# Convolution layer, first half: which engine makes the low halves of 14 weight units

## The chip, the cores and the metric

The kernel runs on one core of one Trainium2 chip. The core has five engines that run at the same time and wait for each other through semaphores: TensorE (PE, matrix products), VectorE (DVE), ScalarE (ACT), GpSimd (POOL) and SyncE (SP, which here only issues transfers). The metric is the device time of one execution in microseconds (us), as the median of several runs; lower is better.

## The reference, cut to what matters

The program computes two layers of a transformer-like network on 512 positions of width 1024: a first block (a gated delta-rule mixer, memory attention, a SwiGLU network), then a convolution layer with its SwiGLU network, then an attention layer with its own. The change touches the first half of the convolution layer: the product with `pw1_w`, the gate, and the depthwise convolution over 31 positions.

```python
def conformer_conv(x, norm_g, pw1_w, pw1_b, dw_w, dw_b, ln_g, ln_b, pw2_w, pw2_b):
    a, b = jnp.split(rmsnorm(x, norm_g) @ pw1_w + pw1_b, 2, axis=-1)
    h = a * jax.nn.sigmoid(b)
    h = lax.conv_general_dilated(
        h, dw_w[:, None, :], window_strides=(1,),
        padding=[(CONV_WIDTH - 1, 0)],
        dimension_numbers=('NWC', 'WIO', 'NWC'),
        feature_group_count=h.shape[-1]) + dw_b
    h = jax.nn.silu(layernorm(h, ln_g, ln_b))
    return h @ pw2_w + pw2_b
```

## The kernel before, in words

**Weights.** All weights are float32 and stream through the core in units of 128 output columns (`pw1` has 16 units, each 128x1024 numbers in the on-chip memory). A product of two float32 numbers is made of three reduced-precision products: the high half of the weight by the high half of the input, the high half by the low half, and the low half by the high half (L291, L292, L293; tiles `WR` and `WL` are the halves of the weight, `XR` and `XL` those of the input). So each unit needs two small preparations: the high half `WR` by ScalarE (`split_ahead`, L252) and then the low half `WL = raw - WR` (L256, `low_unit`, on GpSimd in nearly all stages). `raw`, `WR` and `WL` have two slots each. SP may load the unit after next into a slot of `raw` once the low half of the unit in it is made (semaphore `weight_split`); TensorE starts a unit when `weight_split` has counted its low half.

**The convolution stage** works on 8 tiles of 128 channels (`turn` handles two tiles, `j` = 0 and 1; six tiles in a loop and the last two written out). For each tile TensorE makes two units of `pw1` (the gate half and the other half), 24 products each, and 13 of the 31 positions ("taps") of the convolution as 39 products with diagonal matrices (L1596 to L1598). The order on TensorE is: first unit of the next tile, taps of this tile, second unit of the next tile, first unit of the tile after it, taps of the next tile, and so on.

VectorE does the following for each tile, in this order: read both units out of their banks (`c_b` L1714, `c_a` L1716); form the gated row `c_row` (L1719) after ScalarE's sigmoid; then 18 taps, added alternately into `Y` and `c_odd` (L1727, L1729, then 16 times L1731, each a scalar_tensor_tensor whose two tensor inputs both lie in the on-chip memory SBUF); after the third of these the low half `c_lo` of the row (L1735), for which TensorE's taps wait; at the end three additions (L1742, L1745, L1747). Before the change, VectorE also makes the low half of a weight unit after the fifth tap and another after the fifteenth (`unit_low`, L1707), and one ahead of the first tile: 14 of the 16 units of `pw1`. GpSimd makes the first two. Behind the convolution comes `pw2`, whose first two units GpSimd prepares while VectorE is still in the last two tiles.

ScalarE, for each tile: sigmoid of `c_b` (L1649), the high half `c_hi` of the row (L1651), one weight unit's high half (L252), 26 diagonal blocks for the next tile's taps (L1641), another weight unit's high half (L252).

Of the kernel before, what the change touches and what calls it, by code (L numbers as in the profile page):

```python
# [20 lines left out]
F32 = mybir.dt.float32  # L21
F32R = mybir.dt.float32r
ALU = mybir.AluOpType
# [3 lines left out]
P = 128  # L27
# [33 lines left out]
SLOT = 11 * P  # L61
# [77 lines left out]
def program(nc, t, out):  # L139

    with ExitStack() as ctx:
# [4 lines left out]
        def at(name, offset, cols, dt=F32, parts=P):  # L146
            return nc.alloc_sbuf_tensor_at(name, [parts, cols], dt, offset=base + offset)
# [5 lines left out]
        raw = at("raw", 48 * KB, 2 * SLOT)  # L153
        WR = at("WR", 59 * KB, 2 * SLOT, F32R)
        WL = at("WL", 70 * KB, 2 * SLOT, F32R)
# [25 lines left out]
        def param(name, i=0, n=1):  # L181
            first = PARAMS[name][0]
            return params[:, first + i:first + i + n] if isinstance(i, int) else params[:, bass.ds(first + i, n)]
# [3 lines left out]
        def sem(name):  # L187
            return ctx.enter_context(nc.semaphore(name))
# [9 lines left out]
        high_ahead = sem("high_ahead")  # L198
        weight_split = sem("weight_split")
# [54 lines left out]
        def low_unit(seg, slot):  # L254
            here = slice(slot * SLOT, slot * SLOT + seg.kt * P)
            nc.gpsimd.tensor_tensor(WL[:, here], raw[:, here], WR[:, here].bitcast(F32),  # L256
                                    ALU.subtract).then_inc(weight_split, 1)
# [123 lines left out]
        def cols(tile, i, n=SEQ):  # L381
            return tile[:, i * n:(i + 1) * n] if isinstance(i, int) else tile[:, bass.ds(i * n, n)]
# [1198 lines left out]
        def conv_bank(seg, c):  # L1581

            return bank[(seg.tile0 + c) % 2 if c < 2 else 4 + c]
# [111 lines left out]
        def conv_vector(dve, order):  # L1695
            seg = SEG["pw1"]
            V = nc.vector
            dve.wait_ge(norm_ready, NORM["h2"] + 1)
            clear_sum_now(dve, order, "h2")
            N = TAPS - PE_TAPS  # L1700

            def unit_low(i, c):

                dve.wait_ge(high_ahead, i * 4 + (seg.ahead0 + c + 1))
                slot = (seg.unit0 + c) % 2
                here = slice(slot * SLOT, slot * SLOT + seg.kt * P)
                V.tensor_tensor(WL[:, here], raw[:, here], WR[:, here].bitcast(F32), ALU.subtract).then_inc(weight_split, 1)  # L1707

            def turn(i, last=False):
                for j in range(2):  # L1710
                    n = i * 2 + j
                    row, y = c_row[j], cols(Y, n)
                    dve.wait_ge(unit_done, n * 2 + (seg.unit0 + 1))
                    V.tensor_tensor(c_b[:, :], conv_bank(seg, 2 * j)[:, :], R[:, :], ALU.mult).then_inc(tile_taken, 1)  # L1714
                    dve.wait_ge(unit_done, n * 2 + (seg.unit0 + 2))
                    V.tensor_tensor(c_a[:, :], conv_bank(seg, 2 * j + 1)[:, :], R[:, :], ALU.mult).then_inc(tile_taken, 1)  # L1716
                    dve.wait_ge(tile_taken, n * 2 + (seg.tile0 + 2))
                    dve.wait_ge(glu_gate, n + 1)
                    V.scalar_tensor_tensor(row[:, PAD + 2:ROW], c_a[:, :], param("pw1_a", n), c_b[:, :], ALU.add, ALU.mult).then_inc(glu_ready, 1)  # L1719
                    dve.wait_ge(glu_ready, n + 1)  # L1720
                    for m in range(N):
                        k = PE_TAPS + m
                        src, w, into = row[:, 2 + k:2 + k + SEQ], param("conv31", n * TAPS + k), (y, c_odd[:, :])[m % 2]
                        if m >= 2:
                            dve.wait_ge(tap_added, n * N + (m - 1))
                        if m == 0:
                            ins = V.tensor_scalar(into, src, w, param("dw_b", n), ALU.mult, ALU.add)  # L1727
                        elif m == 1:
                            ins = V.tensor_scalar(into, src, w, None, ALU.mult)  # L1729
                        else:  # L1730
                            ins = V.scalar_tensor_tensor(into, src, w, into, ALU.mult, ALU.add)  # L1731
                        ins.then_inc(tap_added, 1)
                        if m == 2:
                            dve.wait_ge(row_high, n + 1)
                            V.tensor_tensor(c_lo[j][:, PAD + 2:ROW], row[:, PAD + 2:ROW], c_hi[j][:, PAD + 2:ROW].bitcast(F32),  # L1735
                                            ALU.subtract).then_inc(row_low, 1)
                        elif m == 4 and not (last and j):
                            unit_low(i, 2 * j + 3)
                        elif m == N - 4 and not last:
                            unit_low(i, 2 * j + 4)  # L1740
                    dve.wait_ge(tap_added, n * N + N)
                    V.tensor_tensor(y, y, c_odd[:, :], ALU.add).then_inc(odd_added, 1)  # L1742
                    dve.wait_ge(taps_done, n + 1)
                    dve.wait_ge(odd_added, n + 1)
                    V.tensor_tensor(y, y, bank[4 + j][:, :], ALU.add).then_inc(taps_joined, 1)  # L1745
                    dve.wait_ge(taps_joined, n + 1)
                    V.tensor_tensor(ACC[:, :], ACC[:, :], y, ALU.add).then_inc(mean_added, 1)  # L1747
                    dve.wait_ge(mean_added, n + 1)

            unit_low(0, 2)  # L1750
            with dve.Fori(0, DT // 2 - 1) as i:
                turn(i)
            turn(DT // 2 - 1, last=True)
            dve.wait_ge(mean_done, 1)
            V.tensor_scalar(R[:, :], bank[3][:, :], 1.0 / D, None, ALU.mult).then_inc(mean_ready, 1)
            dve.wait_ge(mean_ready, 1)
            with dve.Fori(0, DT) as n:
                V.tensor_tensor(cols(Y, n), cols(Y, n), R[:, :], ALU.subtract).then_inc(centred, 1)
            dve.wait_ge(norm_ready, NORM["var"] + 1)

            def scale(n, j):

                V.tensor_tensor(c_t[j // 2][:, j % 2 * SEQ:(j % 2 + 1) * SEQ], cols(Y, n), R[:, :], ALU.mult).then_inc(ln_scaled, 1)

            def low(n, j):
                dve.wait_ge(input_high, n + (INPUT["conv"] + 1))
                V.tensor_tensor(cols(ML, n), c_t[j // 2][:, j % 2 * SEQ:(j % 2 + 1) * SEQ], cols(MR, n).bitcast(F32), ALU.subtract).then_inc(input_ready, 1)  # L1767

            for n in range(4):
                scale(n, n)  # L1770
            for n in range(DT):
                low(n, n % 4)
                if n + 4 < DT:
                    dve.wait_ge(input_ready, INPUT["conv"] + n + 1)
                    scale(n + 4, n % 4)
            stream_vector(dve, order, SEG["pw2"], "h3", "h3", "ffn1", bias="pw2_b")

        def clear_sum_now(dve, order, norm):
            dve.wait_ge(summed, DT * (NORM[norm] + 1))
            order.link(nc.vector.memset(ACC[:, :], 0.0))  # L1780
# [576 lines left out]
        @block.gpsimd  # L2357
        def _(pool):
            for name in layers:
                seg = SEG[name]  # L2360
                if name in SHARED:
                    for c in range(2):
                        if seg.handed:
                            if name == "pw2" and c == 0:
                                pool.wait_ge(weight_split, seg.unit0)
                            pool.wait_ge(high_ahead, seg.ahead0 + c + 1)
                            low_unit(seg, (seg.unit0 + c) % 2)
                        else:
                            split_unit(pool, seg, seg.unit0 + c, (seg.unit0 + c) // 2, (seg.unit0 + c) % 2)
                    if name == "pw1":  # L2370
                        continue
                    with pool.Fori(1, seg.units // 2) as i:
                        for c in range(2):
                            pool.wait_ge(high_ahead, i * 2 + (seg.ahead0 + c + (1 if seg.handed else -1)))
                            low_unit(seg, (seg.unit0 + c) % 2)
                else:
                    stream(pool, seg, lambda unit, row, turn, slot, seg=seg: split_unit(pool, seg, unit, turn, slot))
# [172 lines left out]
```

## Time and profile before

| | |
|---|---|
| median of 3 runs | 2224.09 us (2220.82 to 2227.03) |
| profiled execution | 2224.37 us, span of its records 2222.6 us |
| PE busy | 2123.2 us, 96% of the span |
| VectorE busy | 1155.7 us, 52% |
| GpSimd busy | 776.0 us, 35% |
| granted TensorE clock, mean | 0.98 |

The shares are means over stages with different limits. The stage of the change lasts from about 937 to 1098 us after the span's start; a row that gives a stretch and each engine's busy time in it is read against the length of the stretch. A row of the timeline gives the start, the duration, the engine, the line and the instruction.

### The profile page before, as it was taken

To read this page: it belongs to the slowest core of one execution; us is meant where nothing else is said; L and a number is where in the kernel's file an instruction comes from. 1 tells how busy PE (TensorE), PEld (TensorE's weight loads), DVE (VectorE), ACT (ScalarE), POOL (GpSimd) and SP (SyncE) were. 2 spreads that over 40 slices of the span, in tenths; PEclk is the share of its full clock that TensorE was granted. 3 is DMA by queue.
4 is the path that set the end of the run, shared out by engine and by line. 5 is a ranking of instruction groups with operands and counts; after the bars stand their busy time and mean duration, and the time that the engine had idled before them with its cause. 6 is when DMAs were issued, how large, how long until landed. Compare 5 with 4: busy or idle time off the path is not lost.

```text
span 2222.6 us, 32867 instructions
## 1 busy us (share of the span) xinstructions
PE 2123.2 (96%) x11682; PEld 1707.8 (77%) x11682; DVE 1155.7 (52%) x1855; ACT 851.6 (38%) x1517; POOL 776.0 (35%) x336
## 2 busy tenths in 40 slices
PE   7899999998999999899889999999999999999997
PEld 4787887766888888688567888888877667888886
DVE  5667798444333322499863333325577854333322
ACT  4334344244332222555353233322566643222321
POOL 3643242223444444100134444444411124444442
PEclk9999999999999999999899999999999999999999
DMA  4321121022333333111113333332200013333322
GB/s 142 103 69 47 41 68 39 30 81 80 91 98 94 94 106 103 48 58 48 37 59 93 95 99 98 120 104 70 67 20 19 19 38 95 94 94 95 111 95 77
DMA packets 44084, 168.98 MB, mean 76 GB/s; under 512 B 4896, under 2 KB 4960, under 8 KB 43616
## 3 DMA queue, kind: packets, MB, share of 16 engines
q1 hardware_dynamic: 43488, 163.59, 24.0%
q10 hardware_dynamic: 512, 4.24, 0.5%
q8 instruction: 56, 0.92, 0.2%
q14 instruction: 28, 0.23, 0.0%
HBM read 165.72 MB, written 2.10 MB: 76 GB/s over the span
## 4 chain that ended last, share of the span: by engine, by line
PE 81%; DVE 7%; issue 6%; ACT 3%; POOL 1%; DVEq 0%; DMA 0%; ACTq 0%; POOLq 0%
PE bank L291 22%; PE bank L293 22%; PE bank L292 22%; PE bank L2099 2%; PE bank L784 2%; PE bank L2054 1%; POOL WL L256 1%; PE bank L2080 1%; PE bank L1596 1%; PE bank L1598 1%; PE bank L1597 1%; ACT Pr L2156 1%; PE bank L774 1%; PE bank L317 1%; DVE c_odd L1731 1%
## 5 line engine op out<-in xcount | busy, mean ns | idle before, releaser
L256 POOL TENSOR_TENSOR WL<-raw,WR 128x1024 fp32r<-128x1024 f32 (+2 forms) x274 | 711.6, 2597 | 1010.3 <-ACT WR L252 1005.6
L291 PE MATMUL bank<-XR,WR 128*128 128x512 f32 x1528 | 616.0, 403 | 21.5 <-DVE XL L452 12.5
L293 PE MATMUL bank<-XR,WL 128*128 128x512 f32 x1528 | 597.5, 391 | 0.0
L292 PE MATMUL bank<-XL,WR 128*128 128x512 f32 x1528 | 597.4, 391 | 0.0
L252 ACT ACTIVATE WR<-raw 128x1024 fp32r<-128x1024 f32 (+2 forms) x230 | 256.2, 1114 | 771.7 <-PE bank L293 764.9
L291 PEld LDWEIGHTS bank<-XR,WR 128*128 128x128 f32 x1528 | 288.6, 189 | 95.6 <-issue 25.9
L291 PE MATMUL bank<-MR,WR 128*128 128x512 f32 (+1 forms) x856 | 336.7, 393 | 15.0 <-DVE ML L1767 6.7
L292 PEld LDWEIGHTS bank<-XL,WR 128*128 128x128 f32 x1528 | 288.6, 189 | 65.0 <-issue 7.7
L293 PEld LDWEIGHTS bank<-XR,WL 128*128 128x128 f32 x1528 | 288.3, 189 | 61.2
L293 PE MATMUL bank<-MR,WL 128*128 128x512 f32 (+1 forms) x856 | 331.9, 388 | 0.0
L292 PE MATMUL bank<-ML,WR 128*128 128x512 f32 (+1 forms) x856 | 331.8, 388 | 0.0
L236 POOL CAST WR<-raw 128x1024 fp32r<-128x1024 f32 (+1 forms) x58 | 64.3, 1108 | 411.9 <-PE bank L293 354.8
L1552 DVE TENSOR_TENSOR f_up<-bank,R 128x512 f32<-128x512 f32 x66 | 45.6, 692 | 306.0 <-PE bank L293 306.0
L291 PEld LDWEIGHTS bank<-MR,WR 128*128 128x128 f32 x856 | 162.7, 190 | 53.0 <-issue 10.9
L293 PEld LDWEIGHTS bank<-MR,WL 128*128 128x128 f32 x856 | 162.5, 190 | 32.7
L292 PEld LDWEIGHTS bank<-ML,WR 128*128 128x128 f32 x856 | 163.0, 190 | 31.1 <-issue 0.2
L1557 DVE TENSOR_TENSOR ML<-f_mid,MR 128x512 f32 x66 | 123.9, 1877 | 64.5 <-ACT MR L1534 64.5
L423 DVE TENSOR_TENSOR ACC<-ACC,SQ 128x512 f32<-128x512 f32 (+1 forms) x49 | 77.9, 1591 | 129.4 <-ACT SQ L412 128.7
L1494 DVE TENSOR_TENSOR hT<-bank,hT 128x512 f32 (+1 forms) x24 | 16.6, 692 | 161.1 <-PE bank L293 161.1
L1550 DVE TENSOR_TENSOR f_gate<-bank,R 128x512 f32<-128x512 f32 x66 | 45.6, 692 | 88.4 <-PE bank L293 73.0
L2156 ACT ACTIVATE Pr<-Pr,stats 128x512 f32<-128x512 f32 (+3 forms) x128 | 70.4, 551 | 44.0 <-DVE stats L2244 44.0
L452 DVE SCALAR_TENSOR_TENSOR XL<-hT,params,XR (+1 forms) x40 | 69.4, 1735 | 32.8 <-ACT XR L448 32.7
(305 smaller groups left out, 2426.6 us busy)
## 6 DMA issues: line engine op xcount, KB each, us to landing
raw<-w SPq DMA_DIRECT2D x224, 512.0 KB, 3.6
raw<-w SPq DMA_DIRECT2D x48, 704.0 KB, 4.1
raw<-w SPq DMA_DIRECT2D x16, 384.0 KB, 3.1
hT<-xT SPq DMA_DIRECT2D x4, 512.0 KB, 5.7
hT<-xT ACTq DMA_DIRECT2D x1, 2048.0 KB, 8.1
out<-Y SPq DMA_DIRECT2D x8, 256.0 KB, 2.0
memT<-memT ACTq DMA_DIRECT2D x1, 1024.0 KB, 5.0
phi<-phi ACTq DMA_DIRECT2D x1, 1024.0 KB, 6.3
```

The costliest lines, as they stand in the source:

```text
L236: nc.gpsimd.tensor_copy(WR[:, here], raw[:, here]).then_inc(high_split, 1)
L252: nc.scalar.activation(WR[:, here], raw[:, here], ACT.Identity).then_inc(high_ahead, 1)
L256: nc.gpsimd.tensor_tensor(WL[:, here], raw[:, here], WR[:, here].bitcast(F32), ALU.subtract).then_inc(weight_split, 1)
L291: nc.tensor.matmul(into, wr, xr(k0 + k), start=start, stop=False)
L292: nc.tensor.matmul(into, wr, xl(k0 + k), start=False, stop=False)
L293: mm = nc.tensor.matmul(into, wl, xr(k0 + k), start=False, stop=stop)
L423: nc.vector.tensor_tensor(ACC[:, 0:width], ACC[:, 0:width], SQ[:, parity * SEQ:parity * SEQ + width], ALU.add).then_inc(summed, 1)
L452: nc.vector.scalar_tensor_tensor(dst, src, gain, high.bitcast(F32), ALU.mult, ALU.subtract).then_inc(input_ready, 1)
L1550: nc.vector.tensor_tensor(f_gate[:, :], bank_of(seg, 2 * p)[:, :], R[:, :], ALU.mult).then_inc(tile_taken, 1)
L1552: nc.vector.tensor_tensor(f_up[:, :], bank_of(seg, 2 * p + 1)[:, :], R[:, :], ALU.mult).then_inc(tile_taken, 1)
L1557: nc.vector.tensor_tensor(cols(ML, n), f_mid[:, :], cols(MR, n).bitcast(F32), ALU.subtract).then_inc(mid_low, 1)
L2156: ins = nc.scalar.activation(here, here, ACT.Exp, bias=stat(idx, 0)[:, b:b + 1], scale=-1.0, accum_out=stat(idx, 1)[:, b:b + 1])
```

## The change

The 14 low halves go from VectorE to GpSimd: `unit_low` and its calls are gone, and GpSimd's loop, which skipped `pw1`, now runs over it as over the other stages. ScalarE, TensorE and the transfers keep their instructions and their order.

```diff
@@ conv_vector
-            def unit_low(i, c):
-
-                dve.wait_ge(high_ahead, i * 4 + (seg.ahead0 + c + 1))
-                slot = (seg.unit0 + c) % 2
-                here = slice(slot * SLOT, slot * SLOT + seg.kt * P)
-                V.tensor_tensor(WL[:, here], raw[:, here], WR[:, here].bitcast(F32), ALU.subtract).then_inc(weight_split, 1)
-
...
-                        elif m == 4 and not (last and j):
-                            unit_low(i, 2 * j + 3)
-                        elif m == N - 4 and not last:
-                            unit_low(i, 2 * j + 4)
...
-            unit_low(0, 2)
             with dve.Fori(0, DT // 2 - 1) as i:
                 turn(i)
@@ gpsimd
                         if seg.handed:
-                            if name == "pw2" and c == 0:
-                                pool.wait_ge(weight_split, seg.unit0)
                             pool.wait_ge(high_ahead, seg.ahead0 + c + 1)
                             low_unit(seg, (seg.unit0 + c) % 2)
...
-                    if name == "pw1":
-                        continue
                     with pool.Fori(1, seg.units // 2) as i:
                         for c in range(2):
                             pool.wait_ge(high_ahead, i * 2 + (seg.ahead0 + c + (1 if seg.handed else -1)))
                             low_unit(seg, (seg.unit0 + c) % 2)
```

On VectorE, in the loop over tiles of the convolution stage, from the third tap of a tile on, the kernel before has (`c_row`, `c_lo`, `c_hi` are one tile's row and its halves, the number behind a name is its buffer):

```order
L1731 SCALAR_TENSOR_TENSOR Y<-c_row_129,params,Y 128x512
L1735 TENSOR_TENSOR c_lo_136<-c_row_129,c_hi_134 128x512
L1725 REGISTER_ALU
L1731 ISA
L1731 SCALAR_TENSOR_TENSOR c_odd<-c_row_129,params,c_odd 128x512
L1725 REGISTER_ALU
L1731 ISA
L1731 SCALAR_TENSOR_TENSOR Y<-c_row_129,params,Y 128x512
L1704 ISA
L1707 TENSOR_TENSOR WL<-raw,WR 128x1024
```

At the same place the changed kernel has:

```order
L1724 SCALAR_TENSOR_TENSOR Y<-c_row_129,params,Y 128x512
L1728 TENSOR_TENSOR c_lo_136<-c_row_129,c_hi_134 128x512
L1718 REGISTER_ALU
L1724 ISA
L1724 SCALAR_TENSOR_TENSOR c_odd<-c_row_129,params,c_odd 128x512
L1718 REGISTER_ALU
L1724 ISA
L1724 SCALAR_TENSOR_TENSOR Y<-c_row_129,params,Y 128x512
L1718 REGISTER_ALU
L1724 ISA
L1724 SCALAR_TENSOR_TENSOR c_odd<-c_row_129,params,c_odd 128x512
```

The weight's low half behind the fifth tap is gone, and the taps behind `c_lo` follow one another without anything between them, up to the addition at the tile's end.

On GpSimd, between `down1` (the product ahead of the convolution layer, units of 128x1408) and the loop of `pw2`, the kernel before has the first two units of `pw1` and the first two of `pw2` one behind the other, then the loop over the rest of `pw2`:

```order
L256 TENSOR_TENSOR WL<-raw,WR 128x1024 x4
L2372 UNCONDITIONAL_BRANCH
L2372 ISA
L256 TENSOR_TENSOR WL<-raw,WR 128x1024
L2374 REGISTER_ALU
```

The changed kernel has there:

```order
L256 TENSOR_TENSOR WL<-raw,WR 128x1024 x2
L2356 UNCONDITIONAL_BRANCH
L2356 ISA
L256 TENSOR_TENSOR WL<-raw,WR 128x1024
L2358 REGISTER_ALU
L256 TENSOR_TENSOR WL<-raw,WR 128x1024
L2356 REGISTER_ALU
L2356 COMPARE_AND_BRANCH
L256 TENSOR_TENSOR WL<-raw,WR 128x1024 x2
```

The row of four is parted, and between the two pairs stands a loop of seven turns with two low halves each, the 14 that VectorE made before.

## Rows read from the trace of the kernel before

**Rows 1.** The page, part 1: busy us (share), instructions.
```profile
PE 2123.2 (96%) x11682; PEld 1707.8 (77%) x11682; DVE 1155.7 (52%) x1855; ACT 851.6 (38%) x1517; POOL 776.0 (35%) x336
```

**Rows 2.** Stretches of one tile each: length, then PE, PEld, DVE, ACT, POOL busy.
```profile
959.62:979.63 20.01, 20.01 (x89) 16.36 (x88) 18.54 (x27) 10.88 (x30) 0.00 (x0) 1.00 0.19 54
979.63:999.28 19.65, 19.65 (x87) 16.08 (x86) 18.54 (x27) 10.87 (x30) 0.00 (x0) 1.00 0.19 54
...
1039.02:1058.85 19.83, 19.83 (x88) 16.22 (x87) 18.62 (x27) 10.88 (x30) 0.00 (x0) 1.00 0.18 53
1058.85:1079.16 20.31, 20.31 (x90) 16.59 (x89) 19.58 (x27) 10.88 (x30) 5.25 (x1) 1.00 0.11 33
1079.16:1098.09 18.93, 11.67 (x43) 8.73 (x41) 18.46 (x25) 3.58 (x4) 2.77 (x1) 0.91 0.14 48
```

**Rows 3.** Line L1707, count and duration in ns, min/median/max.
```profile
L1707 DVE TENSOR_TENSOR WL<-raw,WR x14: 1217/1222/1226, 937.3 to 1065.0; 128x1024 fp32r<-128x1024 f32 x14
```

**Rows 4.** Timeline of VectorE in tile 1: start, duration.
```profile
959.62 0.69 DVE L1714 TENSOR_TENSOR c_b<-bank,R 128x512 f32<-128x512 f32 x1
...
963.22 0.74 DVE L1731 SCALAR_TENSOR_TENSOR Y<-c_row,params,Y 128x512 f32 x1
963.88 0.68 DVE L1735 TENSOR_TENSOR c_lo<-c_row,c_hi 128x512 fp32r<-128x512 f32 x1
964.49 0.74 DVE L1731 SCALAR_TENSOR_TENSOR c_odd<-c_row,params,c_odd 128x512 f32<-128x512 f32 x1
...
965.81 1.22 DVE L1707 TENSOR_TENSOR WL<-raw,WR 128x1024 fp32r<-128x1024 f32 x1
966.95 0.74 DVE L1731 SCALAR_TENSOR_TENSOR c_odd<-c_row,params,c_odd 128x512 f32<-128x512 f32 x1
...
976.82 0.69 DVE L1742 TENSOR_TENSOR Y<-Y,c_odd 128x512 f32 x1
...
978.34 0.69 DVE L1747 TENSOR_TENSOR ACC<-ACC,Y 128x512 f32<-128x512 f32 x1
979.63 0.69 DVE L1714 TENSOR_TENSOR c_b<-bank,R 128x512 f32<-128x512 f32 x1 [0.60 <-DVE ACC L1747]
```

**Rows 5.** Timeline of TensorE in tile 1: unit, taps, next unit begin.
```profile
954.33 0.39 PE L291 MATMUL bank<-XR,WR 128*128 128x512 f32 x1
...
965.23 0.40 PE L1596 MATMUL bank<-c_hi,diag 128*128 128x512 f32 x1
...
974.33 0.39 PE L291 MATMUL bank<-XR,WR 128*128 128x512 f32 x1
```

**Rows 6.** Waits between 890 and 1130 us: total, times, longest.
```profile
PE bank L1596 <- DVE c_lo L1735: 4.8, 2, 4.0
```

**Rows 7.** Timeline of VectorE in the last two tiles.
```profile
1059.99 0.69 DVE L1716 TENSOR_TENSOR c_a<-bank,R 128x512 f32<-128x512 f32 x1 [0.45 <-PE bank L293]
...
1074.04 0.76 DVE L1731 SCALAR_TENSOR_TENSOR c_odd<-c_row,params,c_odd 128x512 f32<-128x512 f32 x1
1074.83 2.77 DVE L1742 TENSOR_TENSOR Y<-Y,c_odd 128x512 f32<-128x512 f32 x1
...
1083.11 0.68 DVE L1735 TENSOR_TENSOR c_lo<-c_row,c_hi 128x512 fp32r<-128x512 f32 x1
1083.71 2.85 DVE L1731 SCALAR_TENSOR_TENSOR c_odd<-c_row,params,c_odd 128x512 f32<-128x512 f32 x1
```

**Rows 8.** Timeline of GpSimd between 1070 and 1086 us.
```profile
1071.81 5.25 POOL L256 TENSOR_TENSOR WL<-raw,WR 128x1024 fp32r<-128x1024 f32 x1 [158.15 <-ACT WR L252]
1083.24 2.77 POOL L256 TENSOR_TENSOR WL<-raw,WR 128x1024 fp32r<-128x1024 f32 x1 [6.19 <-ACT WR L252]
```

**Rows 9.** Timeline of ScalarE in tile 1: the high halves of two units.
```profile
962.62 1.05 ACT L252 ACTIVATE WR<-raw 128x1024 fp32r<-128x1024 f32 x1
...
971.18 1.05 ACT L252 ACTIVATE WR<-raw 128x1024 fp32r<-128x1024 f32 x1
```

**Rows 10.** GpSimd's line L256 beside an idle VectorE, at 1130 us.
```profile
1130.01 2.40 POOL L256 TENSOR_TENSOR WL<-raw,WR 128x1024 fp32r<-128x1024 f32 x1 [44.00 <-ACT WR L252]
```

## The prediction

> **What bounds the kernel now.** The page says that TensorE is busy for 96% of the span and VectorE for 52% [rows 1], but these are means over all stages, so I read the stretches of single tiles in the stage of the change, from one `c_b` to the next. The reader is to see that both engines are nearly full there: from 959.62 to 979.63 us TensorE is busy for 20.01 of 20.01 us, and VectorE for 18.54 [rows 2]. The five tiles between 959.62 and 1058.85 us take 99.23 us, 19.85 each, and TensorE sets that pace: in the timeline VectorE's next `c_b` comes 0.60 us late at 979.63 us [rows 4]. But a tile in which VectorE does not wait takes 19.65 us (979.63 to 999.28) [rows 2]. So VectorE has 0.2 us to spare in a tile, no more. In the last tile the roles change: TensorE has only 11.67 of 18.93 us to do, VectorE 18.46 [rows 2]; VectorE ends the stage.
>
> The second thing to read is what GpSimd and VectorE do to each other. GpSimd has nothing to do in the middle tiles, and one low half in each of the last two [rows 2, 8]. In both cases a VectorE instruction beside it is long: the addition L1742 takes 2.77 us instead of 0.69, and a tap (L1731) 2.85 instead of 0.74 [rows 4, 7]. Both end 0.5 us after GpSimd's instruction ends (1071.81 + 5.25 = 1077.06, and 1083.24 + 2.77 = 1086.01) [rows 7, 8]. GpSimd too is held up: alone it takes 2.40 us [rows 10], here 5.25, and 5.25 - 2.40 = 2.85 us is about the time until VectorE's gapless chain of taps has ended at 1074.80. So the two instructions do not run side by side, one waits for the other. VectorE pays 2.77 - 0.69 = 2.08 and 2.85 - 0.74 = 2.11 us; I take 2.10 for one low half made by GpSimd while VectorE is dense in taps.
>
> **The change, part by part.** It removes 14 instructions of 1.22 us from VectorE [rows 3]. In the chain each costs 966.95 - 965.81 = 1.14 us, since neighbours overlap a little [rows 4]. One, at 937.3 us, is ahead of the first tile, where VectorE next waits for ScalarE's sigmoid, so it counts nothing; GpSimd will make it while VectorE is idle. The other 13 stand in the tiles: two in each of tiles 0 to 5, one in tile 6, none in tile 7.
>
> It adds 13 instructions of 2.40 us on GpSimd, which was idle, so their length itself costs nothing. The price is what they hold up. When do they come? GpSimd starts as soon as ScalarE's high half is there. In tile 1 these end at 962.62 + 1.05 = 963.67 and 971.18 + 1.05 = 972.23 us [rows 9]. Both times lie inside VectorE's run of two-input instructions: the first between the third tap and `c_lo` (963.22 and 963.88), the second among the late taps, before L1742 at 976.82 [rows 4]. The first is placed almost as in tile 7, where GpSimd got its turn between `c_lo` and the next tap; the second as in tile 6, where it got it ahead of L1742 [rows 7, 8]. So each of the 13 stops VectorE for 2.10 us where it used to work for 1.14: 0.96 us more.
>
> A tile of VectorE then takes 19.65 + 2 x 0.96 = 21.57 us. TensorE's tile has no more work than before (19.85), so VectorE becomes the bound, and TensorE waits about 1.7 us in each tile, at the taps, for `c_lo`. Today it reaches the taps at 965.23 us, 0.67 us after `c_lo` ends (963.88 + 0.68) [rows 4, 5], and it waited for `c_lo` only twice [rows 6].
>
> The sum, along VectorE from the first tile to the last:
> - tile 0: 2 x 0.96 = 1.9 us;
> - tiles 1 to 5: 21.57 instead of 19.85, 5 x 1.72 = 8.6 us;
> - tile 6: 0.96 for its one low half, less the 0.45 us for which it waits for TensorE now [rows 7], which the delay swallows: 0.5 us;
> - tile 7: nothing moves, its GpSimd instruction was there before: 0.
>
> Together 11.0 us. What follows (the mean, the variance, `pw2`) hangs on VectorE's last addition and moves by as much. Profiled time 2224.37 + 11.0 = 2235.4 us; the profiled execution is 0.3 us above the median of 2224.09, so the two can be used alike.
>
> Should the first GpSimd instruction get in ahead of `c_lo` instead of behind it, VectorE's sum is the same, but TensorE's taps start 2.1 us later. Its way from there is 9.1 us of taps (974.33 - 965.23) and one unit of about 5.45 (half of 965.23 - 954.33) [rows 5], 14.6 us until the other half of the next tile is ready; VectorE needs from the end of `c_lo` (964.56) to the end of L1747 (979.03) 14.5 us less 2.3 for the low halves plus 2.1 for one stop, 14.3 [rows 4]. They come out equal, so nothing is added to within 0.5 us.
>
> The second unit's low half is late, but in time: it ends about 2.3 us after the last tap, and TensorE needs it 14.6 us after `c_lo`. VectorE's 15 taps from `c_lo` on take 15 x 0.66 = 9.9 us (the pace from 963.22 to 963.88), one stop 2.1: 14.3 us [rows 4]. The slot of `raw` comes free some 4 us later than now; the next high half in that slot is due two halves later, a whole tile, so that is covered.
>
> The price of one stop is bounded thus: from below 0 (GpSimd falls into a wait of VectorE; these are 0.3 to 0.6 us long), from above the whole 2.40 us of a GpSimd instruction [rows 10] plus the 0.5 us until VectorE's instruction ends, less its own 0.7: 2.2 us. I take 2.10, since both rows that show it in this very code say so. The Trainium skill states such a rule ("SBUF — State Buffer", section "SBUF: two separate sides"): VectorE and GpSimd share a pair of ports under an exclusive lock, held for the whole instruction, and a VectorE instruction with two SBUF inputs takes it against a GpSimd instruction that reads SBUF. By that rule a VectorE instruction due at the moment when GpSimd starts would lose all 2.40 us, and the sum would be 13 x (2.40 - 1.14) = 16.4 less the 1.5 us of slack, about 15 us. The trace agrees with the lock, but not with "whichever starts first": GpSimd's instruction of 1071.81 us was passed over by four more taps.
>
> **The rivals.** *GpSimd is starved.* The instruction of 1071.81 us did not get in between taps, only where the chain had a gap at 1074.80 [rows 7, 8]. If the first low half of a tile misses its chance around `c_lo`, it waits through all 15 taps, 9.9 us, and ends 9.9 + 2.3 = 12.2 us after `c_lo`. TensorE wants that unit when its taps are done, 9.3 us after `c_lo`: it waits 3.0 us in each of 7 tiles, some 21 us in all, 2245.4 us. It speaks for it that ScalarE ends only 0.2 us ahead of `c_lo` [rows 4, 9], against it that in tile 7 GpSimd started 0.13 us after `c_lo` and still got the turn behind it [rows 7, 8]. Chance 0.13.
>
> *No change (the other side).* If a stop costs little because GpSimd mostly fits where VectorE waits or reads banks, VectorE keeps its tile under 19.85 us. That decides at 19.65 - 2.28 + 2s = 19.85, a stop s of 1.24 us. Then TensorE sets the pace as now, and only tile 6 may gain its 1.14 us: about 2223.3 us. It can't be much faster, since TensorE is full in tiles 1 to 6. Against it stand both rows of 2.1 us. Chance 0.14, with the cases up to 6.7 us slower (a stop of some 1.8 us).
>
> *The raw slots come free late and the loads delay ScalarE's high halves.* A few us more than forecast at most, since a tile's length lies between; 0.05, and its time of some 2238 us is in the range.
>
> **How the numbers follow.** My forecast has 0.68, and by itself 2231 to 2239 us (stops of 1.9 to 2.3 us, slack 1 us either way). The range reaches up to the starved case and a little down for cheaper stops: 2229 to 2247. Below it stays most of the no-change case. About 0.3% (6.7 us) is what a measurement of this kernel can tell from no change. Faster by that much has hardly a mechanism, 0.04; within 0.3% 0.16; slower 0.80.
>
> **What the profile after would show.** GpSimd has 14 more instructions of L256 between 935 and 1065 us, several of them well over 2.40 us. VectorE has two instructions of 2.8 us in each of tiles 0 to 5, one beside `c_lo` and one at L1742. The stretch from one `c_b` to the next is 21.5 us, and TensorE waits 1 to 2 us for `c_lo` at L1596 in every tile. Starvation would show as one GpSimd instruction of 10 us or more in each tile, and TensorE waiting at L291 for `WL`. The forecast is wrong if VectorE's long instructions are absent, or if tiles take 20 us in spite of them.

## The result, and the profile after

The changed kernel takes 2236.73 us (median of 12 runs, 2231.16 to 2241.01), the kernel before 2223.15 us (median of 12): a ratio of 1.0057, 95% interval 1.0044 to 1.007. Slower by 13.6 us; 11.0 were forecast. The profiled execution took 2237.62 us, its span is 2235.8 us, 13.2 more than before.

Page of the changed kernel, span and part 1 (compare [rows 1]):

```profile
span 2235.8 us, 32882 instructions
...
PE 2128.1 (95%) x11682; PEld 1711.7 (77%) x11682; DVE 1167.3 (52%) x1841; ACT 851.7 (38%) x1517; POOL 838.7 (38%) x350
```

VectorE lost 14 instructions and is busy 11.6 us longer (1167.3 against 1155.7). Instructions are gone, and what the others take longer is more than those took.

Stretches of the changed kernel from one `c_b` to the next, tiles 1 to 7 (length, then PE, PEld, DVE, ACT, POOL busy, granted TensorE clock; compare [rows 2]):

```profile
961.35:983.29 21.94, 20.67 (x90) 16.65 (x89) 20.46 (x25) 10.87 (x30) 9.67 (x2) 1.00 0.18 55
983.29:1004.86 21.57, 19.75 (x79) 15.71 (x78) 20.46 (x25) 10.88 (x30) 9.63 (x2) 0.92 0.15 41
...
1048.48:1070.14 21.66, 21.66 (x96) 17.62 (x95) 20.48 (x26) 10.87 (x30) 9.69 (x2) 1.00 0.17 50
1070.14:1091.22 21.08, 18.51 (x80) 14.53 (x78) 20.48 (x25) 10.88 (x30) 9.11 (x2) 1.00 0.17 48
1091.22:1110.14 18.92, 11.79 (x39) 9.11 (x39) 18.35 (x25) 3.58 (x4) 2.77 (x1) 0.82 0.14 46
```

The five tiles from 961.35 to 1070.14 us take 108.79 us, 21.76 each, where they took 19.85. Tile 6 takes 21.08 instead of 20.31, tile 7 18.92 instead of 18.93.

Timeline of VectorE in tile 1 of the changed kernel (compare [rows 4]):

```profile
965.61 0.68 DVE L1728 TENSOR_TENSOR c_lo<-c_row,c_hi 128x512 fp32r<-128x512 f32 x1
966.21 2.88 DVE L1724 SCALAR_TENSOR_TENSOR c_odd<-c_row,params,c_odd 128x512 f32<-128x512 f32 x1
969.01 0.74 DVE L1724 SCALAR_TENSOR_TENSOR Y<-c_row,params,Y 128x512 f32 x1
...
978.40 2.77 DVE L1731 TENSOR_TENSOR Y<-Y,c_odd 128x512 f32 x1
981.28 0.69 DVE L1734 TENSOR_TENSOR Y<-Y,bank 128x512 f32 x1
...
983.29 0.69 DVE L1707 TENSOR_TENSOR c_b<-bank,R 128x512 f32<-128x512 f32 x1 [0.60 <-DVE ACC L1736]
```

Timeline of GpSimd in the same tile (compare [rows 8]):

```profile
965.47 3.08 POOL L256 TENSOR_TENSOR WL<-raw,WR 128x1024 fp32r<-128x1024 f32 x1 [6.32 <-ACT WR L252]
974.03 6.59 POOL L256 TENSOR_TENSOR WL<-raw,WR 128x1024 fp32r<-128x1024 f32 x1 [5.49 <-ACT WR L252]
```

The tap behind `c_lo` is held for 2.88 - 0.74 = 2.14 us, and L1731, the first of the three additions at the tile's end, for 2.77 - 0.69 = 2.08 us; so it is in each of tiles 0 to 5, to within 0.02 us. GpSimd's second low half is passed over by six taps that start behind it and takes 6.59 us. TensorE's waits for `c_lo` between 890 and 1145 us (total, times, longest; compare [rows 6]) have grown with it:

```profile
PE bank L1596 <- DVE c_lo L1728: 14.0, 6, 6.3
```

### The profile page after: what moved, and what is told of

It reads as the page before. It is cut to its first block, busy times and chain, and to the rows that moved or that the text cites. A ratio compares the mean times of both kernels' runs of the same rounds, so it can differ in the third digit from the quotient of the medians.

```text
span 2235.8 us, 32882 instructions
## 1 busy us (share of the span) xinstructions
PE 2128.1 (95%) x11682; PEld 1711.7 (77%) x11682; DVE 1167.3 (52%) x1841; ACT 851.7 (38%) x1517; POOL 838.7 (38%) x350
## 4 chain that ended last, share of the span: by engine, by line
PE 76%; DVE 10%; issue 8%; ACT 3%; POOL 1%; DVEq 0%; DMA 0%; ACTq 0%; POOLq 0%; SPq 0%
PE bank L291 22%; PE bank L293 21%; PE bank L292 21%; PE bank L2087 2%; DVE c_odd L1724 2%; PE bank L784 2%; PE bank L2042 1%; POOL WL L256 1%; PE bank L2068 1%; DVE Y L1731 1%; DVE Y L1724 1%; ACT Pr L2144 1%; PE bank L774 1%; PE bank L317 1%; DVE Pr L2275 0%
## 5 line engine op out<-in xcount | busy, mean ns | idle before, releaser
L256 POOL TENSOR_TENSOR WL<-raw,WR 128x1024 fp32r<-128x1024 f32 (+2 forms) x288 | 775.6, 2693 | 954.7 <-ACT WR L252 950.1
```

## Experiments

All times are medians, ratios against the kernel before, whose medians beside these runs were 2221.9 to 2223.2 us. "Tile" is the mean of the five stretches from `c_b` of tile 1 to `c_b` of tile 6.

**Half of the change: the first low half of each tile.** `e1_first_half`:

```diff
+                dve.wait_ge(weight_split, i * 4 + (seg.unit0 + c))
...
-                        elif m == 4 and not (last and j):
-                            unit_low(i, 2 * j + 3)
...
+                        with pool.Fori(1, seg.units // 2) as i:
+                            pool.wait_ge(high_ahead, i * 2 + (seg.ahead0 + 2))
+                            pool.wait_ge(weight_split, i * 2 + (seg.unit0 + 1))
+                            low_unit(seg, (seg.unit0 + 1) % 2)
```

> In each tile the first of the two low halves (behind c_lo) is made by GpSimd, the second stays on VectorE. Theory (each stop costs VectorE 2.10 us in place of 1.14): a tile of VectorE grows from 19.83 to 20.79 us, TensorE's is 20.0; seven stops, together about +6.2 us against the kernel before, ratio about 1.0028; one VectorE instruction of 2.9 us in each tile, behind c_lo. Rival (the second low half is what costs, since GpSimd is passed over for four taps and more and ends late): no difference from the kernel before, within 2 us.

**The other half: the second low half of each tile.** `e1b_second_half`:

```diff
+                dve.wait_ge(weight_split, i * 4 + (seg.unit0 + c))
...
-                        elif m == N - 4 and not last:
-                            unit_low(i, 2 * j + 4)
...
-            unit_low(0, 2)
...
+                        with pool.Fori(1, seg.units // 2) as i:
+                            pool.wait_ge(high_ahead, i * 2 + (seg.ahead0 + 1))
+                            pool.wait_ge(weight_split, i * 2 + seg.unit0)
+                            low_unit(seg, seg.unit0 % 2)
```

> The other half of the change alone: the second low half of each tile (and the one ahead of the first tile) on GpSimd, the first stays on VectorE. Theory: six stops at the last addition of tiles 0 to 5, +0.96 us each, about +5.5 us, ratio about 1.0025; the two halves add up to the whole change. Rival (only GpSimd's lateness costs): all of the 13 us of the change are here.

Measured: 2232.11 us (1.0041, 1.0025 to 1.0057) and 2230.87 us (1.0036, 1.0022 to 1.0051). The tile is 20.82 us in the first (104.11 / 5, from 960.39 to 1064.50 us) and 20.76 in the second (103.79 / 5, from 961.62 to 1065.41). Each stop thus adds 0.9 to 1.0 us to the tile, the two are alike, and together they give the 21.76 of the whole change. VectorE's last addition ends 6.4 and 6.3 us later than before, where 6.2 and 5.5 were expected; the medians are 9.0 and 7.7 us up, 2.6 and 1.4 us more than that (see "Behind the stage" below). The rival that all the cost is GpSimd's lateness in the second half is out.

**Nobody makes the 14 low halves.** `e2_none`; the products with them use what lies in the slot, so that part of the result is left out:

```diff
-        def low_unit(seg, slot):
+        def low_unit(seg, slot, make=True):
...
+            if not make:
+                nc.gpsimd.sem_inc(weight_split, 1)
+                return
...
-                            low_unit(seg, (seg.unit0 + c) % 2)
+                            low_unit(seg, (seg.unit0 + c) % 2, make=name != "pw1")
```

> Nobody makes the 14 low halves: GpSimd only counts them as made (the products with them use what lies in the slot from earlier units, so this part of the result is left out). Theory: without GpSimd's instructions there are no stops, VectorE's tile is 19.83 - 2.28 = 17.6 us, TensorE sets the pace with 20.0 as before; 1.1 us below the kernel before (ratio 0.9995) and 14 us below the changed one. Rival (something in the new order of waits costs, not the instruction beside the taps): well above the kernel before.

Measured: 2221.91 us (0.9996, 0.9984 to 1.0009). The order of waits of the changed kernel costs nothing; GpSimd's instructions cost it all, 14.8 us against the changed kernel's median. It also shows how little there was to win: with the low halves for nothing TensorE still sets the pace. From tile 1 to tile 5 `c_lo` starts every 20.00 us (962.20 to 1042.20), and VectorE waits for TensorE at `c_a` (total, times, longest, between 890 and 1145 us):

```profile
DVE c_a L1712 <- PE bank L296: 16.3, 7, 2.8
```

**Sums of the taps in PSUM.** `e3_sums_in_psum`, a tap then reads one operand from SBUF and one from PSUM:

```diff
-                        src, w, into = row[:, 2 + k:2 + k + SEQ], param("conv31", n * TAPS + k), (y, c_odd[:, :])[m % 2]
+                        src, w, into = row[:, 2 + k:2 + k + SEQ], param("conv31", n * TAPS + k), bank[2 + m % 2][:, :]
...
-                            ins = V.scalar_tensor_tensor(into, src, w, into, ALU.mult, ALU.add)
+                            ins = V.scalar_tensor_tensor(y if m == N - 2 else into, src, w, into, ALU.mult, ALU.add)
...
-                    V.tensor_tensor(y, y, c_odd[:, :], ALU.add).then_inc(odd_added, 1)
+                    V.tensor_tensor(y, y, bank[3][:, :], ALU.add).then_inc(odd_added, 1)
```

> The changed kernel with VectorE's two running sums of the taps in PSUM banks 2 and 3, so that a tap reads one operand from SBUF and one from PSUM. Theory (GpSimd and a VectorE instruction with two SBUF inputs keep each other out): no tap and not the addition at the tile's end is long any more; but GpSimd is now not kept out by the third tap either and gets in ahead of c_lo, which has two SBUF inputs: c_lo takes 2.8 to 3.0 us, and TensorE waits for it. The way from c_lo over taps, one unit, c_a and back to c_lo is 14.9 + 4.35 + 2.2 = 21.4 us, so the time stays near that of the changed kernel, +8 to +12 us against before less up to 4 us for the two stops in the last two tiles that vanish. Rival (any VectorE instruction is stopped, whatever it reads): taps of 2.9 us remain as they are, and the time is that of the changed kernel.

Measured: 2232.78 us (1.0051, 1.0036 to 1.0067), tile 21.53 us (107.64 / 5). Timeline of VectorE in tile 1 of this kernel:

```profile
966.34 2.33 DVE L1728 TENSOR_TENSOR c_lo<-c_row,c_hi 128x512 fp32r<-128x512 f32 x1
968.60 2.72 DVE L1724 SCALAR_TENSOR_TENSOR bank<-c_row,params,bank 128x512 f32<-128x512 f32 x4
```

and of GpSimd at the same time:

```profile
965.74 2.39 POOL L256 TENSOR_TENSOR WL<-raw,WR 128x1024 fp32r<-128x1024 f32 x1 [11.83 <-ACT WR L252]
```

The taps are 0.75 us each throughout, and GpSimd takes its 2.4 us everywhere, whether or not VectorE works. But `c_lo`, which still reads two SBUF tiles, is held until 0.5 us after GpSimd's end. The stops of the taps are gone and the time isn't: the single hold now falls on the one instruction for which TensorE waits, and the way `c_lo`, taps, unit, `c_a`, `c_lo` sets the tile. From tile 1 to tile 5 one `c_lo` follows another in 21.26 to 21.30 us, where 21.4 was worked out; the mean of 21.53 has in it tile 1 with 22.94 us, in which `c_a` waits 3.22 us for TensorE (a stretch of lower clock in tile 0, granted 0.62 from 946.00 to 949.40 us, is part of that).

**GpSimd waits for `c_lo` as well.** `e3w_psum_and_wait`:

```diff
+                            if name == "pw1" and c == 1:
+                                pool.wait_ge(row_low, i)
```

> The changed kernel with the tap sums in PSUM, and GpSimd starts the first low half of a tile only after c_lo (a wait on row_low). Theory: no VectorE instruction of tiles 0 to 6 is long, neither tap nor c_lo; VectorE's tile is 17.6 us, TensorE sets the pace with 20.0 us; the stop of tile 7 is gone too (2.1 us): about 2221 us, ratio 0.999, 15 us below the changed kernel. Rival (GpSimd stops VectorE in any instruction, or TensorE waits for weights made too late): tiles of more than 21 us and a time near the changed kernel's.

**The kernel before with its sums in PSUM**, low halves on VectorE, `e4_psum_old_engine` (the edit of the sums alone):

> The kernel before, low halves on VectorE, with the tap sums in PSUM. Theory: tiles as before (VectorE 19.83, TensorE 20.0 us), only the stop of tile 7 vanishes: about 2221 us, the same as with the low halves on GpSimd behind c_lo; so PSUM sums alone are worth nothing in the middle tiles, and what they do for the changed kernel is that they take its stops away. Rival (a tap with its sum in PSUM is itself faster or slower than 0.66 us): a difference of more than 5 us either way.

Measured: 2222.64 us (1.0002, 0.999 to 1.0013) and 2226.16 us (1.0013, 1.0003 to 1.0024). The tile of the first is 20.18 us (100.90 / 5), and it is 14 us below the changed kernel: with no VectorE instruction held in the middle tiles, moving the low halves is free. Against the second kernel, which has its sums in PSUM too, the move even gains: 3.5 us by the medians. Both were expected at about 2221; they came out 1.6 and 5.2 us above it. Of this the traces show three parts. With the taps in PSUM, GpSimd's instruction for the second unit of `pw2` is not kept out by the third tap of tile 7, and it holds that tile's `c_lo` (2.51 us in both). In the profiled execution of the first, which at 2228.46 us is 5.8 us above its own median, TensorE waits 2.21 us for the first `c_lo`, to 945.65 us, and its clock is low behind it; whether this was so in the other executions is not shown. TensorE's timeline from there:

```profile
945.65 0.76 PE L1596 MATMUL bank<-c_hi,diag 128*128 128x512 f32 x1 [2.21 <-DVE c_lo L1728]
946.21 0.63 PE L1597 MATMUL bank<-c_lo,diag 128*128 128x512 f32 x1
946.64 0.63 PE L1598 MATMUL bank<-c_hi,diag 128*128 128x512 f32 x1
```

Two stretches of the same kernel (length, then PE, PEld, DVE, ACT, POOL busy, granted clock):

```profile
945.65:949.06 3.41, 3.41 (x8) 2.70 (x9) 3.41 (x6) 3.41 (x13) 2.38 (x1) 0.52 0.00 0
949.06:955.00 5.94, 5.94 (x27) 4.83 (x26) 5.94 (x10) 3.62 (x11) 2.25 (x1) 1.00 0.33 91
```

For 3.4 us the products come every 0.43 us instead of 0.23, the lower of the two clock levels; that is about 1.5 us on the path of a kernel that TensorE bounds. The kernel before and `e4_psum_old_engine` waited 0.81 and 1.31 us at that place, and their clock did not fall there; but `e11_after_14_taps` waited 2.31 us there and its clock did not fall either (granted 1.00 from 945.66 to 949.06 us). In the second kernel, tiles are 20.22 us (101.10 / 5), 0.4 above before: the first two taps (tensor_scalar) cost 0.81 and 0.74 us with PSUM as their output, against 0.55 and 0.48. So PSUM sums alone are a small loss.

**Two taps more on VectorE.** `e5_psum_11_taps`, the version with the wait, and:

```diff
-        PE_TAPS = 13
+        PE_TAPS = 11
```

> As the one with the sums in PSUM and the wait for c_lo, and two taps move from TensorE to VectorE (11 and 20 in place of 13 and 18). Theory: TensorE's tile is 20.0 - 1.4 = 18.6 us, VectorE's 17.6 + 1.3 = 18.9 us; seven tiles some 1.1 us shorter, the last one 1.3 us longer and without its stop: about 7.5 us below the kernel before, 2215.5 us, ratio 0.9965. Rival (the stage's length is not set by these two engines' tiles): no gain, 2221 to 2224 us.

Measured: 2217.97 us (0.9982, 0.9971 to 0.9993). The tile is 19.27 us (96.37 / 5), 0.6 below before, where 18.9 us was expected (the slower tensor_scalars again, 0.5 us together), and tile 7's `c_lo` still took 2.51 us.

**A gap in the chain of taps.** `e6_one_gap`, on the changed kernel:

```diff
-                            dve.wait_ge(tap_added, n * N + (m - 1))
+                            dve.wait_ge(tap_added, n * N + (m - (0 if m == 13 else 1)))
```

> The changed kernel with one more wait on VectorE: tap 13 of a tile waits for tap 12 to have ended, which makes a gap of some 0.03 us in the chain of taps, 3 us ahead of its end. Theory (GpSimd gets its turn only where VectorE's instructions leave a gap): GpSimd's second low half takes 3 to 4 us in place of 6.6, tap 13 is the long instruction and not the tile's last addition, and the time stays within 2 us of the changed kernel's. Rival (GpSimd can't get in between taps at all): 6.6 us and the long addition stay.

Measured: 2237.26 us (1.0066, 1.005 to 1.0082). VectorE around tap 13 (counted from 0) of tile 1:

```profile
975.60 0.73 DVE L1724 SCALAR_TENSOR_TENSOR Y<-c_row,params,Y 128x512 f32 x1
976.48 2.68 DVE L1724 SCALAR_TENSOR_TENSOR c_odd<-c_row,params,c_odd 128x512 f32<-128x512 f32 x1
...
981.84 0.69 DVE L1731 TENSOR_TENSOR Y<-Y,c_odd 128x512 f32 x1
```

GpSimd's second low half in the same tile:

```profile
975.31 3.30 POOL L256 TENSOR_TENSOR WL<-raw,WR 128x1024 fp32r<-128x1024 f32 x1 [5.49 <-ACT WR L252]
```

GpSimd's second low half takes 3.3 us instead of 6.6, the held instruction moves from the last addition to tap 13, and the time stays. When GpSimd gets in changes nothing for VectorE; that it gets in costs 2 us. A gap in the chain is enough for GpSimd to get its turn.

**Each low half in two pieces.** `e7_two_halves`, on the changed kernel:

```diff
+                            if name == "pw1":
+                                mid = (seg.unit0 + c) % 2 * SLOT + 4 * P
+                                here = slice(mid - 4 * P, mid)
+                                nc.gpsimd.tensor_tensor(WL[:, here], raw[:, here], WR[:, here].bitcast(F32), ALU.subtract)
+                                here = slice(mid, mid + 4 * P)
+                                nc.gpsimd.tensor_tensor(WL[:, here], raw[:, here], WR[:, here].bitcast(F32),
+                                                        ALU.subtract).then_inc(weight_split, 1)
+                                continue
```

> The changed kernel with each of GpSimd's 14 low halves in two instructions of 512 columns. Theory (GpSimd gets a turn only at c_lo and at a gap, and is passed over inside the chain of taps): the first piece gets in behind c_lo and holds a tap for half as long, 1.6 us in place of 2.9; the second piece waits until the tile's last addition, some 10 us, so TensorE waits about 3 us for its weights at L291 in every tile: about 20 us above the kernel before, 2242 to 2247 us, the starved case of the prediction. Rival (GpSimd gets in at any tap once it has waited long enough): both pieces are done within 5 us of c_lo, and the time is that of the changed kernel, 2236.

Measured: 2230.05 us (1.0034, 1.0021 to 1.0048), 7 us below the changed kernel. The theory fell, and of the rival only half came true: the first pair of pieces is done within 3 us of the end of `c_lo`, but the time is not that of the changed kernel. VectorE in tile 1:

```profile
966.08 1.78 DVE L1724 SCALAR_TENSOR_TENSOR c_odd<-c_row,params,c_odd 128x512 f32<-128x512 f32 x1
967.79 1.79 DVE L1724 SCALAR_TENSOR_TENSOR Y<-c_row,params,Y 128x512 f32 x1
969.50 0.74 DVE L1724 SCALAR_TENSOR_TENSOR c_odd<-c_row,params,c_odd 128x512 f32<-128x512 f32 x1
...
978.22 1.67 DVE L1731 TENSOR_TENSOR Y<-Y,c_odd 128x512 f32 x1
980.00 0.69 DVE L1734 TENSOR_TENSOR Y<-Y,bank 128x512 f32 x1
980.72 0.87 DVE L1736 TENSOR_TENSOR ACC<-ACC,Y 128x512 f32<-128x512 f32 x1
```

GpSimd in tile 1, two instructions to a low half:

```profile
965.34 1.97 POOL L2362 TENSOR_TENSOR WL<-raw,WR 128x512 fp32r<-128x512 f32 x1 [4.81 <-ACT WR L252]
967.27 1.75 POOL L2364 TENSOR_TENSOR WL<-raw,WR 128x512 fp32r<-128x512 f32 x1
973.91 5.42 POOL L2362 TENSOR_TENSOR WL<-raw,WR 128x512 fp32r<-128x512 f32 x1 [4.89 <-ACT WR L252]
979.31 1.74 POOL L2364 TENSOR_TENSOR WL<-raw,WR 128x512 fp32r<-128x512 f32 x1
```

The second piece did not starve: a tap that has itself been held is followed by GpSimd's turn, though tap follows tap there without a gap. In the quiet chain at 973.91 us GpSimd is passed over again, and so it is in tiles 0, 2, 4 and 5. Not in tile 3, where it comes at the same point of the same chain, 0.22 us ahead of a tap (8.44 us behind the start of `c_lo`, 8.43 in tile 1), and that very tap is held:

```profile
1015.13 0.74 DVE L1724 SCALAR_TENSOR_TENSOR c_odd<-c_row,params,c_odd 128x512 f32<-128x512 f32 x1
1015.80 1.77 DVE L1724 SCALAR_TENSOR_TENSOR Y<-c_row,params,Y 128x512 f32 x1
```

and GpSimd at the same time:

```profile
1015.58 1.45 POOL L2362 TENSOR_TENSOR WL<-raw,WR 128x512 fp32r<-128x512 f32 x1 [4.89 <-ACT WR L252]
```

So a quiet chain mostly passes GpSimd over, but not always, and nothing in the trace tells the two cases apart. The gain is in the second pair: its second piece runs beside L1734, which reads a PSUM bank, writes SBUF and isn't held (0.69), and holds only the next addition by 0.87 - 0.69 = 0.18 us. The holds of a tile add up to 1.04 + 1.05 + 0.98 + 0.18 = 3.25 us instead of 4.22, and the tile is 20.96 us (104.80 / 5; tile 3, where both pieces held a tap, took 21.94, the others 20.6 to 21.0).

**The last `c_lo` let go first.** `e9_pw2_wait_too`, the version with 11 taps, and:

```diff
+                            if name == "pw2" and c == 1:
+                                pool.wait_ge(row_low, DT)
```

> As the one with 11 taps, and GpSimd's low half of the second unit of pw2, which held up the last c_lo (2.51 us), also waits for c_lo. Theory: c_lo of tile 7 takes 0.7 us, the stage ends 1.8 us earlier: about 2216 us, the lowest of all. Rival (the end of the stage is set by TensorE's taps or by the load of the weights): the same 2218.

**12 taps on TensorE**, `e10_12_taps`:

> The same with 12 taps on TensorE and 19 on VectorE. TensorE's tile 19.3 us, VectorE's 18.5 (measured 19.2 with 20 taps, less 0.66): TensorE sets the pace, 19.3 against 19.2 us, the last tile 0.66 us shorter: within 1 us of the version with 11 taps.

Measured: 2217.10 us (0.9978, 0.9967 to 0.9988) and 2218.49 us (0.9979, 0.9969 to 0.9988). In the first, tile 7 from `c_b` to the end of the last addition takes 18.87 us instead of 20.69 in the kernel with 11 taps alone, the 1.8 us that were expected; of the median only 0.9 us is to be seen, less than these runs can tell. `c_lo` in tile 7:

```profile
1075.64 0.68 DVE L1728 TENSOR_TENSOR c_lo<-c_row,c_hi 128x512 fp32r<-128x512 f32 x1
```

and GpSimd's instruction behind it:

```profile
1076.47 2.38 POOL L256 TENSOR_TENSOR WL<-raw,WR 128x1024 fp32r<-128x1024 f32 x1 [10.30 <-DVE c_lo L1728]
```

Both versions beat the kernel before and the changed one; between the two there is no difference.

**One tap more on TensorE in the changed kernel.** `e11_after_14_taps`, `PE_TAPS = 14` and nothing else:

> The changed kernel with one tap more on TensorE (14) and one less on VectorE (17), nothing else. Theory (VectorE is the bound in the changed kernel, 21.76 us a tile, TensorE has 20.0): VectorE's tile is 21.1, TensorE's 20.7; eight tiles 0.66 us shorter: about 5 us below the changed kernel, 2231.5 us. Rival (what holds the changed kernel is TensorE and its waits for c_lo): TensorE's tile grows by 0.7 and the time with it, 2241 us.

Measured: 2230.90 us (1.004, 1.0025 to 1.0055), 5.8 us below the changed kernel; tile 21.11 us (105.53 / 5). More work for the engine that is busy 95% of the time makes the kernel faster: VectorE bounds this stage.

## Why the prediction was right

**The stop and its price (2.10 us where 1.14 was worked).** Right. Measured 2.14 and 2.08 us: two in each of tiles 0 to 5 and one more than before in tile 6, at the places named. `e2_none` takes the cost away with the instructions, `e1_first_half` and `e1b_second_half` split it into equal shares, `e3_sums_in_psum` and `e3w_psum_and_wait` show that a tap with its sum in PSUM is not held. That it is the input that counts, and not the output that went to PSUM with it, is seen in `e7_two_halves` at L1734, which reads PSUM, writes SBUF and takes its 0.69 us beside GpSimd.

**The Trainium skill's rule** ("SBUF — State Buffer", section "SBUF: two separate sides") says that a VectorE instruction with two SBUF inputs and a GpSimd instruction that reads SBUF exclude each other, and by that rule one with a PSUM input does not; the traces of the PSUM versions agree (taps of 0.75 us beside GpSimd's 2.40). The same sentence of the page says that the one that "starts first gets the pair for the whole instruction". By the profile's start times that is not so in a chain: six taps that started behind GpSimd's instruction of 974.03 us went ahead of it.

**The sum.** Worked out 11.0 us, measured in the stage 1110.14 - 1098.09 = 12.05 us at VectorE's last addition. Tile 0: 1.9 forecast, 1.7 measured (961.35 - 959.62); the two stops give 1.95 from its `c_lo` on, and the low half ahead of it, counted as nothing, gave back 0.2, since `c_lo` starts at 944.12 us instead of 944.34. Tile 6: 0.5 and 0.8; of the 0.45 us of waiting only 0.2 was swallowed (from `c_b` to `c_lo` 3.96 us instead of 4.18). Tile 7: 0 and 0. The term that was mis-sized is tiles 1 to 5, 8.6 us forecast and 108.79 - 99.23 = 9.6 measured. The step behind it was "in the timeline VectorE's next `c_b` comes 0.60 us late at 979.63 us", which I read as a wait for TensorE, with 19.65 us as a tile that does not wait. In the changed kernel the same row reads 0.60 again, at 983.29 us, while it is TensorE that waits for VectorE; every run has such an idle time of 0.56 to 0.60 us ahead of `c_b` of tiles 2 and 4, where VectorE's own loop over two tiles turns. So a tile of VectorE's own was the mean of such a pair, 19.85, and not 19.65. TensorE did have a pace of its own in the kernel before, but it was 20.00 us: its taps begin at 965.23 us and then every 20.00 us up to tile 6.

```profile
985.23 0.40 PE L1596 MATMUL bank<-c_hi,diag 128*128 128x512 f32 x1
...
1005.23 0.40 PE L1596 MATMUL bank<-c_hi,diag 128*128 128x512 f32 x1
```

VectorE, late from tile 0, caught up on that at 0.15 us a tile, and the first wait for TensorE that the timeline shows is 0.28 us, in tile 5:

```profile
1039.99 0.69 DVE L1716 TENSOR_TENSOR c_a<-bank,R 128x512 f32<-128x512 f32 x1 [0.28 <-PE bank L293]
```

So in tiles 1 to 5 there was next to nothing that a delay could swallow: 19.85 + 2 x 0.96 = 21.77, measured 21.76. The forecast of 11.0 against 13.6 is near because the price of a stop, its larger part, was right.

**Behind the stage** I forecast nothing. There the profile gives 13.2 - 12.05 = 1.1 us more. From the last addition to the first `c_t` the changed kernel is 1.5 us shorter, with a higher granted clock in that stretch. The kernel before:

```profile
1098.09:1114.76 16.67, 12.51 (x18) 3.94 (x18) 5.60 (x11) 6.34 (x11) 0.00 (x0) 0.69 0.00 1
```

The changed kernel:

```profile
1110.14:1125.36 15.22, 11.02 (x18) 3.67 (x18) 5.60 (x10) 6.34 (x11) 0.00 (x0) 0.78 0.00 1
```

Later, up to the attention stage, 1.4 and 1.1 us come back, in two steps. The same two steps stand in the traces of `e2_none` and `e3w_psum_and_wait`, in which no instruction of the middle tiles is held, and of `e4_psum_old_engine`; in others only the first, or none. So they come and go without the change and I don't count them to it; whether they explain the 2.6 and 1.4 us by which the medians of the two half changes exceed their stages is not shown.

**The rival of starvation** (0.13) did not come true: in every tile the first low half got in behind `c_lo`. That GpSimd can be passed over was right (6.6 us), but not how I had pictured it, as `e7_two_halves` showed: after a held tap it got its turn at once, and once (tile 3) in a quiet chain too. What decides was not settled. I had the turn behind `c_lo` from one row of tile 7 and gave no cause for it, so that it came out so in every tile is in part luck. **The rival of no change** fell with its condition, since every stop was above 1.24 us. TensorE's wait for `c_lo`, forecast at 1 to 2 us in every tile, came in five of tiles 0 to 6, 1.05 to 1.83 us long (in tile 7 it is 6.31 us, 3.99 before). Tiles 3 and 5 have none, and the tiles before them show why: behind the waits of 1.82 and 1.83 us in tiles 2 and 4 TensorE's clock was lower for 3.4 us, the 39 products of the taps took 10.7 us instead of 9.15, and TensorE came to the next taps no earlier than `c_lo`. Stretches of 3.4 us behind a wait in the changed kernel, tile 0 (a wait of 1.76 us) and tile 2 (1.82 us); the granted clock is the third number from the right:

```profile
944.95:948.35 3.40, 3.40 (x15) 2.78 (x16) 3.40 (x3) 3.40 (x13) 2.11 (x1) 1.00 0.03 8
988.48:991.88 3.40, 3.40 (x9) 2.67 (x10) 3.40 (x3) 3.40 (x13) 2.09 (x1) 0.55 0.11 10
```

## What to carry to other kernels

Before work goes from VectorE to GpSimd, look at what VectorE's neighbours read: beside instructions with two SBUF inputs GpSimd's work isn't free but costs VectorE nearly the length of GpSimd's instruction (2.1 us of its 2.40, and 1.04 of the 1.30 us that a piece of 512 columns takes at 936 us in `e7_two_halves`, beside no such instruction), here to save 1.14. If it must move, first put one of the operands into PSUM, and then see which two-input instruction is left and who waits for it; make GpSimd wait until that one is through. And an idle time that comes at each turn of an engine's loop, in every run with the same length, is the loop's own and not slack to be used up; here it was 0.60 us, put down to VectorE's own last instruction in most runs and to TensorE in `e4_psum_old_engine` and `e5_psum_11_taps`, so the releaser named doesn't tell.

## What the runs showed of the hardware that was not expected

- Who is next between GpSimd and a chain of overlapping taps is not simply a matter of who started first: a chain passed over GpSimd six times (6.6 us instead of 2.4), a gap of 0.15 us let it in (3.3 us), and so did the end of `c_lo` and of a tap that had been held; and in one tile of `e7_two_halves` an undisturbed chain let it in at the point at which the chains of the other tiles passed it over.
- A wait of TensorE was followed by 3.4 us at the lower clock level in some places and not in others, and the length of the wait alone does not say where: it was so behind 1.82 and 1.83 us in tiles 2 and 4 of the changed kernel (granted clock 0.55 and 0.66) and behind 2.21 us in tile 0 of `e3w_psum_and_wait` (0.52), and not behind 1.76 us in tile 0 of the changed kernel nor behind 2.31 us in tile 0 of `e11_after_14_taps` (1.00).
- A tensor_scalar of 128x512 float32 took 0.55 and 0.48 us into SBUF and 0.81 and 0.74 us into PSUM; a scalar_tensor_tensor took 0.75 us in both cases.
